# Parting the tokens at 384 in a down projection: five products a weight tile instead of six

## What is computed

```
u = x @ w_up
a, b = u[..., :D_FF], u[..., D_FF:]
h = gelu(conv(a)) * b                 # D_FF = 2816 features
x = layer_norm(ALPHA * x + h @ w_down)  # D_MODEL = 1024
```

## Time and profile before

| | us |
|---|---|
| median of 3 runs | 1924.11 |
| the three runs | 1924.13, 1922.37, 1924.11 |
| the profiled execution's own time | 1922.85 |
| its span, first to last instruction | 1921.1 |
| PE busy in the span | 1865.4 (97%) |
| DVE busy | 1009.3 (53%) |
| ACT busy | 659.7 (34%) |
| POOL busy | 544.4 (28%) |
| mean granted TensorE clock | 0.993 |

### The profile page before, as it was taken

How to read it: one execution, slowest core, us unless ns; L and a number is a source line. 1 busy time by engine, 2 the same in 40 slices (tenths; PEclk the granted TensorE clock), 3 DMA queues, 4 the chain that set the end, 5 groups by cost and what they waited for, 6 DMA issues and landing times.

```text
span 1921.1 us, 32071 instructions
## 1 busy us (share of the span) xinstructions
PE 1865.4 (97%) x12562; PEld 1770.5 (92%) x12562; DVE 1009.3 (53%) x1584; ACT 659.7 (34%) x1388; POOL 544.4 (28%) x241
## 2 busy tenths in 40 slices
PE   7998999999999999999999999999999999999996
PEld 6987888899999999999998888879999999999995
DVE  3466544458854423443674665444597443334447
ACT  3245333432433212332332453334343332133323
POOL 2321111133143334332322311111322332433231
PEclk9999999999999999999999999999999999999998
DMA  6442232232122122111241523223221221222121
GB/s 180 120 144 76 94 105 86 104 121 88 45 88 82 50 88 88 66 70 55 83 137 42 158 69 106 96 74 133 94 82 69 72 74 66 77 88 73 55 73 55
DMA packets 58802, 169.44 MB, mean 88 GB/s; under 512 B 8120, under 2 KB 26216, under 8 KB 50728
## 3 DMA queue, kind: packets, MB, share of 16 engines
q1 hardware_dynamic: 58696, 167.97, 26.3%
HBM read 149.42 MB, written 18.28 MB: 87 GB/s over the span
## 4 chain that ended last, share of the span: by engine, by line
PE 91%; DVE 5%; DMA 2%; POOL 1%; issue 1%; ACT 1%; SPq 0%; ACTq 0%; DVEq 0%; POOLq 0%
PE ps L1514 61%; PE ps L1759 10%; PE ps L1839 3%; PE ps L1548 3%; PE ps L1693 2%; PE ps L1665 2%; PE ps L1561 2%; PE ps L1736 1%; DMA gate_logits<-logits 1%; DVE res L1329 1%; DVE res L1325 1%; PE ps L1672 1%; PE ps L1674 1%; POOL w_lo L648 1%; PE ps L1740 1%; PE ps L1522 1%
## 5 line engine op out<-in xcount | busy, mean ns | idle before, releaser
L648 POOL TENSOR_TENSOR w_lo<-w_raw,w_hi 128x1024 fp32r<-128x1024 f32 (+2 forms) x237 | 544.1, 2304 | 1340.8 <-ACT w_hi L712 1329.8
L712 ACT ACTIVATE w_hi<-w_raw 128x1024 fp32r<-128x1024 f32 (+2 forms) x236 | 225.4, 974 | 465.6 <-PE ps L1514 441.7
L1514 PE MATMUL ps<-x_hi,w_hi 128*128 128x320 f32 x1408 | 321.4, 309 | 0.0
L1514 PE MATMUL ps<-x_lo,w_hi 128*128 128x320 f32 x1408 | 321.0, 309 | 0.0
L1514 PE MATMUL ps<-x_hi,w_lo 128*128 128x320 f32 x1408 | 320.6, 309 | 0.0
L1514 PEld LDWEIGHTS ps<-x_hi,w_lo 128*128 128x128 f32 x1408 | 235.5, 188 | 0.0
L1514 PEld LDWEIGHTS ps<-x_hi,w_hi 128*128 128x128 f32 x1408 | 235.2, 188 | 0.3
L1514 PEld LDWEIGHTS ps<-x_lo,w_hi 128*128 128x128 f32 x1408 | 235.3, 188 | 0.0
L1759 PE MATMUL ps<-x_hi,w_hi 128*128 128x320 f32 x512 | 164.9, 322 | 7.1 <-ACT logits L800 7.1
L1414 DVE TENSOR_SCALAR f_conv<-f_ext,vec 128x656 f32<-128x656 f32 x44 | 64.6, 1469 | 201.8 <-ACT tail L934 199.3
L1759 PE MATMUL ps<-x_hi,w_lo 128*128 128x320 f32 x512 | 159.5, 311 | 0.0
(11 more groups left out here) (255 smaller groups left out, 3206.4 us busy)
## 6 DMA issues: line engine op xcount, KB each, us to landing
w_raw<-in_slabs SPq DMA_DIRECT2D x86, 1024.0 KB, 4.8
w_raw<-in_slabs SPq DMA_DIRECT2D x20, 768.0 KB, 4.0
gate_logits<-logits SPq DMA_DIRECT2D x64, 160.0 KB, 1.9
gates<-gate_logits SPq DMA_DIRECT2D x16, 640.0 KB, 6.2
w_raw<-in_slabs SPq DMA_DIRECT2D x16, 640.0 KB, 3.7
ckvc<-in_ckvc SPq DMA_DIRECT2D x16, 256.0 KB, 2.7
ckvc_t<-in_ckvc_t SPq DMA_DIRECT2D x16, 256.0 KB, 2.9
x_in<-in_x_t SPq DMA_DIRECT2D x4, 640.0 KB, 9.0
```

What stands on the lines that cost most here:

```text
L648: pool.tensor_tensor(w_lo[:, s % 2, c], w_raw[:, s % 2, c], w_hi[:, s % 2, c].bitcast(F32), ALU.subtract).then_inc(wlo_ready, 1)
L712: A(w_hi[:, s % 2, c], w_raw[:, s % 2, c], ACT.Copy).then_inc(whi_ready, 1)
L1514: ins = MM(out_[:, a, :], w, x[:, t, a * HT:(a + 1) * HT], start=t == 0 and w is wh and x is hi, stop=t == tiles - 1 and w is wl)
```

## The change

The first down projection of each layer gets a function of its own, `joint`, in place of `dense`. The tokens are parted at 384 (`FT`): the first bank of a job's pair holds 384 columns, and the second bank holds 512. For each weight tile the first 384 tokens have their three products of 384 columns. The last 256 tokens of `hf_hi` and of `hf_lo` go through `w_hi` in one product of 512 columns, whose moving operand is read in two runs of 256 columns that lie 24 T elements apart, and whose results stand side by side in the second bank. `w_lo` with the last 256 of `hf_hi` is a product of 256 columns into the first half of that bank. That makes five products a weight tile (384, 384, 384, 256 and 512 columns). The halves of the second bank are added when DVE takes the job: `residual` becomes four instructions, with a semaphore, `res_begun`, between the second and the third. `hf_hi` and `hf_lo` are now views of one tensor at the same places as before. Nothing else uses `joint`.

```diff
+FT = T - 256
@@
-        hf_hi = place("hf_hi", 0, [P, F1, T], F32R)
+        hf = place("hf", 0, [P, 3 * F1, T], F32R)
+        hf_hi, hf_lo = hf[:, 0:F1, :], hf[:, 2 * F1:3 * F1, :]
@@
-        hf_lo = place("hf_lo", 24 * T, [P, F1, T], F32R)
@@
+        res_begun = sem("res_begun")
@@
+        def first_cols(n):
+            return ps[:, 2 * (n % 4), 0:FT]
+        def last_cols(n):
+            return ps[:, 2 * (n % 4) + 1, :].rearrange("p (x n) -> p x n", x=2)
@@ def residual(n, k, j, n_loop):
                     dve.wait_ge(job_done, layer * NJ + JC + n_loop + j + 1)
-                    r = row(res, j)
-                    STT(halves(r), halves(row(x_hi, j).bitcast(F32)), ALPHA, pair(n + k), ALU.mult, ALU.add
-                        ).then_inc(job_taken, 1)
+                    r, x = row(res, j), row(x_hi, j).bitcast(F32)
+                    STT(r[:, 0:FT], x[:, 0:FT], ALPHA, first_cols(n + k), ALU.mult, ALU.add)
+                    STT(r[:, FT:], x[:, FT:], ALPHA, last_cols(n + k)[:, 0, :], ALU.mult, ALU.add).then_inc(res_begun, 1)
+                    dve.wait_ge(res_begun, layer * KD + j + 1)
+                    TT(r[:, FT:], last_cols(n + k)[:, 1, :], r[:, FT:], ALU.add).then_inc(job_taken, 1)
                     dve.wait_ge(job_taken, layer * NJ + n_loop + j + 2)
                     STT(r, row(x_lo, j).bitcast(F32), ALPHA, r, ALU.mult, ALU.add).then_inc(res_ready, 1)
@@
+                def joint(n, s, tiles, i, jper, sper, ready):
+                    start_job(n, i, jper)
+                    weights(s, 0, i, sper)
+                    both = hf.rearrange("p (x f) n -> p x f n", x=3)
+                    for t in range(tiles):
+                        if t == tiles // 2:
+                            weights(s, 1, i, sper)
+                        ready(t)
+                        c = t * P
+                        wh, wl = w_hi[:, s % 2, c:c + P], w_lo[:, s % 2, c:c + P]
+                        def both_last():
+                            return MM(last_cols(n), wh, both[:, 0:3:2, t, FT:], start=t == 0, stop=t == tiles - 1)
+                        if t == 0:
+                            both_last()
+                        for x, w in ((hf_hi, wh), (hf_lo, wh), (hf_hi, wl)):
+                            MM(first_cols(n), w, x[:, t, 0:FT], start=t == 0 and w is wh and x is hf_hi,
+                               stop=t == tiles - 1 and w is wl)
+                        MM(last_cols(n)[:, 0, :], wl, hf_hi[:, t, FT:], start=False, stop=False)
+                        if t:
+                            ins = both_last()
+                    ins.then_inc(job_done, 1)
@@ def down_half(s0, job0, nf):
-                            dense(job0 + k, s0 + k, 0, nf, hf_hi, hf_lo, 2, i=i, jper=4, sper=4,
-                                  ready=(lambda t: rows(t, 0)) if k == 0 else None)
+                            joint(job0 + k, s0 + k, nf, i, 4, 4,
+                                  (lambda t: rows(t, 0)) if k == 0 else (lambda t: None))
```

## The result

The changed kernel takes 1927.09 us (median of 22 runs, 1924.35 to 1929.90) against 1924.11 us of the kernel before on the same chips (22 runs, 1920.70 to 1927.81). I had forecast 2.6 us less. The profiled execution of after took 1924.50 us, with a span of 1922.6; the span of before was 1921.1.

A forecast was written before the change was run, and what follows sets the result against it. PE was taken to bound the kernel. 192 fewer products at 13.33 ns gave -2.56 us, all other terms zero, so the median 1924.11 became 1921.55 us (forecast 1921.5); range 1917.9 to 1924.6.

The forecast's parts named there:

- What bounds the kernel: Both first down projections: PE is the whole chain, without holes, 84.48 us a stage, so PE savings move everything behind.
- The price of a product: First down projections: fixed 13.3 ns per fp32r product whatever its width; 192 fewer products save 2.56 us; chance 0.66.
- B: Rival, chance 0.18: extra time goes with columns, so five products cost what six did; 1923.7 to 1924.1 us.
- The fp32 rows: Plain fp32 products of 320 and 512 columns: 0.84 ns a column, only 1 to 2 ns fixed per product.
- The floor of a weight load: Changed stage: a load needs no more than 0.11 us, so 256-column products at 117 to 120 ns hide it; cost zero.
- The order of the products: Changed stage: three successive products accumulating into the same 384 columns, instead of alternating banks, cost zero.
- the operand in two runs: Changed stage: the 512-column product reading its moving operand in two runs was taken to cost zero.
- Rival D: Chance 0.04: the 512-column product's second run is fetched slowly, 107 ns a weight tile, 20.5 us in all; 1942 us.
- DVE: residual per job: some 1.5 us instead of 0.82, 11 us of DVE work in all, none on the chain.
- the slide along POOL's subtraction: DVE's SBUF addition slides 0.7 us, waiting on or holding up POOL by up to 1.5 us; cost zero through slack.
- All behind them hangs on data from them, so the sum passes through: After both layers' stages: their saving reaches the end of the kernel undiminished, -2.56 us.
- SP, ACT and POOL issue what they issued before: Other engines during the changed stages: instructions issued stay the same, so no cost arises there.

The follow-up runs named there:

- one_run: Changed kernel with the 512-column product reading one run of 512 columns instead of two of 256, part of the result left out; 1932.28 us, one execution.
- dve_only: Kernel before, six products kept, DVE taking each job of the first down projection in three instructions with the new wait; 1924.27 us, ratio 0.9998.
- again: The changed kernel unchanged, run once more against the kernel before; 1927.26 us, ratio 1.0018.
- pe_only: Changed kernel without the third DVE instruction of residual and its wait, part of the result missing; 1927.02 us, ratio 1.0014 to before.
- layer0: Kernel before with the change in the first layer only; 1928.30 us, ratio 1.0018.
- shift: Kernel before, all products kept, with 160 unused semaphore increments on PE in the first layer's stage; 1926.95 us, ratio 1.0007.
- pad: Changed kernel with two unused semaphore increments on PE per weight tile of joint, restoring the old program length; 1924.33 us, ratio 1.0000 to before.
- layer1: Kernel before with the change in the second layer only; 1923.65 us, ratio 0.9993.
- early: Kernel before with 80 unused semaphore increments on PE early in the first layer, ahead of its attention; 1923.37 us, ratio 0.9988.

## Why the prediction was wrong

**What bounds the kernel** was read rightly for the stage: PE was the chain, had no hole before and has none after, and what DVE was given cost nothing.

**The price of a product: the step that failed.** I had two readings of 146.67 ns at full clock and 266.7 at half clock, 32 cycles a product or 0.1 cycle a column, with rows that fit both, and took the first as the "simplest reading" at 0.66. One width can't tell a constant from a slope. The fp32 rows, the only ones with two widths, spoke for the slope, and I put them aside because their columns come at half rate. The extra time over one column a cycle grows with the columns: 12 ns at 256, 13 at 320, 16.5 at 384 and 19 at 512. A line through the first and the last would still leave 5 ns to each product, but the stage gives none of it back: a weight tile takes 881 ns against 880. So how far the extra time is strictly B's slope stays open, and that it isn't a saving of 13.3 ns a product is shown. The term was -2.56 us and measured +0.20.

**The floor of a weight load** held: no hint that 256 columns are too few, and 111.6 ns measured for the narrower product. **The order of the products** and **the operand in two runs** cost nothing that the stage's 0.10 us could not hold, as taken; `one_run` bounds the second at zero. Rival D fell.

**DVE** was estimated at 1.5 us to the SBUF addition and measured 1.47. The three instructions measured 0.55, 0.42 and 0.42 us against 0.556 and 0.424. The slide along POOL's subtraction that I allowed for shrank to nothing: the addition began 0.49 us later and ended at the same time.

**"All behind them hangs on data from them, so the sum passes through"**, and "SP, ACT and POOL issue what they issued before": this is the second step that failed, and it costs as much: some 2.8 us that the sum put at nothing (3.0 less the 0.2 of the stages), beside the 2.8 us of the first. It is true of the data. What it leaves out is that PE's program itself comes in pieces by DMA (queue 8), and that a stage with fewer instructions moves the point at which each later piece is fetched. The page of before had the line, 74 packets on an instruction queue, and the prediction passes over it at 0.2% of the engines' time.

**The sum of what was found.** The stages give +0.20 us, shown. The rest lies between the issue of the second layer's first `krc_t` and that layer's changed stage, and the 14 traces show it in two stretches, neither of which holds a product that any of the kernels changed.

| | 8 traces without the collision | 6 traces with it |
|---|---|---|
| from that `krc_t` to the next, us | 14.8 in seven, 16.3 in `dve_only` | 15.55 in `after` and `again`, 16.8 to 19.3 in four |
| from there to the second stage, us | 423.5 to 423.9 | 424.0 to 425.4 |
| both, mean, us | 438.7 | 441.8 |

The first row holds the wait for `krc_t` and, in five traces, a stretch at half clock right behind it: in `pe_only`, `layer0`, `shift` and `one_run` with the collision, and in `dve_only` without. The stretch costs 1.5 us where it is 3.4 us long (16.31 against 14.76 in `dve_only`, 17.01 in `layer0` against 15.55 in `after`), and it is 6.8 us long in `shift` and `one_run`. The second row holds the late `gates` loads. Together the collisions cost 3.1 us on average, with the stages up to 3.3, against 2.5 to 4.3 us (3.1 on average) by the medians of `after`, `again`, `pe_only`, `layer0` and `shift`. The profile of after alone is one of the cheap ones: 0.8 and 0.6 us here and 0.2 in the stages, and its span grew by 1.5 (1922.6 against 1921.1). That the extra time comes with the program's length is shown by `pad`, `layer0`, `layer1` and `shift`. What remains open is how a wait leads to a half-clock stretch, and how often: 4 of 6 against 1 of 8 are counts on few traces, and the first layer has such a stretch in 6 of the 13 traces with its shorter wait, and not in `early`. `layer0`, and the same place in before the second row:

```profile
1175.20:1178.40 3.20, 3.20 (x13) 2.82 (x12) 1.65 (x7) 1.07 (x3) 0.00 (x0) 0.51 0.00 0
```

```profile
1172.00:1176.00 4.00, 3.92 (x28) 3.92 (x28) 2.01 (x9) 1.16 (x5) 0.00 (x0) 1.00 0.00 0
```

The clock is 0.51 against 1.00, after PE had stood for 1.1 us.

**The chances.** The range ended at 1924.6, half a microsecond above B, and the time fell 2.5 us beyond it. B had 0.18 and was right for the stage to 0.1 us. What lies beyond is the cost of the collisions, and no rival of mine held a cost outside the stage at all.

## What to carry to other kernels

A pace measured at one width says nothing of what fewer and wider products bring: get a second width of the same type first, from another stage or from one run. In a kernel with little slack, look where the instruction queue's packets fall beside the loads that an engine waits for; a change of program length upstream can cost or win one to three microseconds there, and a padded copy (the new work at the old length) tells this from the change's own worth. Once such a collision is found it can be moved away by a few instructions that do nothing, as `early` did, though the next edit moves it again.

## What was unexpected of the hardware

- A column of an fp32r product costs 1.09 to 1.11 cycles at 2.4 GHz (256 columns 118.9, 320 146.7, 384 176.5, 512 232.6 ns), and for 320 columns exactly one at 1.2 GHz (266.7 ns). With two-byte numbers 320 columns fall to 135.7 ns, and reading every second number takes half of the gain back (141.7).
- Beside a single packet of program, 16 KB on queue 8, a 64 KB load landed after 6.6 to 8.2 us in place of 6.0 to 6.3, though the packet took under 1% of the engines' time in that stretch. Why so small a packet costs so much is open.
- Instructions that do nothing can make a kernel faster: 80 of them brought the ratio to 0.9988 (0.9979 to 0.9997).
